# A hybrid decoder layer on one core: QKV weight loads one slot earlier, and the second normalised input turned by VectorE and DRAM instead of TensorE

## The chip, the cores and the metric

The kernel runs on one core of a Trainium2 chip. The metric is the device time of one execution in microseconds (us); lower is better. Engines carry the profile's names: PE (TensorE; PEld is its weight load), DVE (VectorE), ACT (ScalarE), POOL (GpSimd), SP (SyncE, which here only issues DMAs).

## The reference, cut to what matters

One decoder layer over 1024 tokens of 1024 channels, in f32. The first part normalises the input and projects it into a recurrent branch (RG-LRU), three groups of dilated window attention and gates. The part that the change's larger half touches is the end:

```
merged = gates[0] * yr + gates[1] * ya
x = x + merged @ w_out
pe = p @ w_ple
pg = sigmoid(rms_norm(x, norm_ple) @ w_ple_gate + b_ple_gate)
x = x + pg * pe
```

`rms_norm(x, gain)` divides each token's row by its root mean square and multiplies by a gain per channel. The product with `w_ple_gate` contracts over channels, so the normalised input must stand with channels on partitions, while the rows come out of the product with `w_out` with tokens on partitions. Something has to turn it.

## The kernel before, in words

**Products.** Every f32 product is three matmuls of rounded halves (`hi*hi`, `hi*lo`, `lo*hi`; lines 1318, 1322, 1323), accumulated in one PSUM bank. Product number n goes to bank n % 4; PE waits until product n - 4 has been taken out (`bank_free`). Banks 4 to 7 serve the other uses.

**Weights.** SP loads a weight piece (128 rows x 512) into one of four raw buffers. POOL cuts it: L599 writes the rounded high half and L595 the rest into a ring. In the QKV stage the ring has 12 slots, later 16. SP may load piece p when piece p - 4 is cut; POOL may cut into a slot when PE has used what was there. POOL works through the pieces in order, with some other work at fixed places between them.

**QKV stage.** Nine chunks of weights, each 8 pieces, and 8 token tiles per chunk: 72 slots of 8 blocks (a block is one piece's three matmuls). Attention steps are strewn among the blocks, one per 6 blocks. `main_order` writes the order of slots and steps out, and each engine follows it. In step A, DVE rotates and normalises q and k of tile A, transposes them in 32 x 32 squares (L1160) and SP turns them over DRAM: four writes of 32 KB (L542), then, when they have landed, a read of 128 KB (L549). PE uses a tile four steps later. `loaded_after(G)` says up to which piece SP has issued loads when it passes slot G of this order: half the next chunk after the chunk's slot 0, all of it after slot 2. SP's loads (L528, later L504) and turns stand in one order on one queue.

Between the first four and the last four pieces of chunks 3 and 4, POOL permutes half of the first normalised input (`permute_hn`, L615, 16 instructions each), which PE needs in pairs from slot 0 and slot 4 of chunk 3 on.

**The end.** `merged` is held as m_hi and m_lo. The product with `w_out` runs over two halves of the columns, 8 token tiles each (`natural`, 24 matmuls a tile). For each tile of the second half:

- DVE adds x (L1262);
- ACT sums the squares and takes the root (L962, L964);
- DVE takes the reciprocal (L1271) and scales the row by it and the gain into `xg` (L1276), two buffers;
- PE transposes tile t - 2 in eight squares into banks 4 and 5 (`xg_transposes`, L1559);
- ACT copies the banks to m_hi (L954), and DVE writes the rest to m_lo (L1250).

Tiles 6 and 7 are transposed among the first tiles of the last stage. There, for two halves of the columns and 8 tiles each, PE makes a gate product (24 matmuls) and a product with `w_ple` (6 matmuls). DVE adds the bias to the gate product (L1287), ACT takes the sigmoid (L972), DVE multiplies by the other product (L1297, which frees its bank) and adds x (L1299), and ACT issues the output DMA.

Of the kernel before, what the change touches and what calls it, by code (L numbers as in the profile page):

```python
# [12 lines left out]
P = 128  # L13
# [40 lines left out]
PIECES = FIRST_TAIL + PIECES_TAIL  # L54
PIECES_Z = (2 * KD + HEADS) * KD // 4
FIRST_O = FIRST_TAIL + PIECES_Z


def ring_slot(p):
# [52 lines left out]
def loaded_after(G):  # L112

    if G < SLOTS_Q:
        c, s = divmod(G, NT)
        return FIRST_QKV + KD * (c + 1) + (KD // 2 if s < 2 else KD)
    return FIRST_TAIL + max(KD, G - SLOTS_Q + 11)

# [1 line left out]
Q_STAT = 15  # L120

P_CUT = (2, 4)

WARM = 16

# [98 lines left out]
def build_layer(nc, a):  # L224
    stack = ExitStack()
    with stack:
        def sem(name):
            return stack.enter_context(nc.semaphore(name))
# [93 lines left out]
        x2 = [at(f"x2_{t}", [P, D], F32, x2_off[t]) for t in range(NT)]  # L322
        xg = [at("xg0", [P, D], F32, X + 40960), at("xg1", [P, D], F32, H + 45056)]
        gain_ple = at("gain_ple", [P, D], F32, X + 45056)
        pT = at("pT", [P, KP, S], F32, H + 40960)
        pT_hi = at("pT_hi", [P, KP, S], F32R, H + 49152)
        pT_lo = at("pT_lo", [P, KP, S], F32R, H + 57344)
# [25 lines left out]
        y_dram = nc.dram_tensor("y_dram", (NJ, 2, P, S), F32, kind="Internal").ap()  # L353
        o_dram = nc.dram_tensor("o_dram", (UNITS, P, S), F32, kind="Internal").ap()
        gate_dram = nc.dram_tensor("gate_dram", (2 * KD, P, S), F32, kind="Internal").ap()
        turn_dram = nc.dram_tensor("turn_dram", (4, 2 * QUADS, QUAD, QUADS, QUAD), F32, kind="Internal").ap()
        stat_dram = nc.dram_tensor("stat_dram", (2, TILES, P), F32, kind="Internal").ap()
        mw_dram = nc.dram_tensor("mw_dram", (GROUPS, HEADS * NT, P), F32, kind="Internal").ap()
# [96 lines left out]
        x2_std = sem("x2_std")  # L455
        half_done = sem("half_done")
        xg_done = sem("xg_done")
        xgT_done = sem("xgT_done")
        xgT_hi_done = sem("xgT_hi_done")
        xgT_lo_done = sem("xgT_lo_done")  # L460
        pre_done = sem("pre_done")
# [39 lines left out]
        @block.sync  # L501
        def _(sp):
            def load(s, src):
                sp.dma_start(raw[:, s], src).then_inc(raw_in[s], 16)  # L504


            for t in range(4):
                sp.dma_start(x_nat[:, t], a["x"][t * P:(t + 1) * P, :]).then_inc(x_in[t], 16)
            for dst, src in ((ident, "ident"), (gain_mix, "gain_mix")):
                sp.dma_start(dst[:], a[src]).then_inc(consts_in, 16)  # L510
            for s in range(RAW):
                load(s, a["w_rnn_s"][s])
            for t in range(4, NT):
                sp.dma_start(x_nat[:, t], a["x"][t * P:(t + 1) * P, :]).then_inc(x_in[t], 16)
            for dst, src in ((bias_in, "bias_in"), (chan, "chan")):
                sp.dma_start(dst[:], a[src]).then_inc(chan_in, 16)
            sp.dma_start(spare_first[:, :, 0], chunk_bias(0).rearrange("p (q i) -> p q i", q=4)).then_inc(bq_in[0], 16)

            def load_pieces(first, end):

                for p in range(first, end):
                    sp.wait_ge(w_ready, p + 1 - RAW)
                    if p < FIRST_QKV:
                        load(p % RAW, a["w_rnn_s"][p])
                    elif p < FIRST_TAIL:
                        c, k = divmod(p - FIRST_QKV, KD)
                        for u, col, width, dst in chunk_sources(c):
                            sp.dma_start(raw[:, p % RAW, dst:dst + width], a["w_qkv_s"][u * KD + k, :, col:col + width]  # L528
                                         ).then_inc(raw_in[p % RAW], 16)
                    else:  # L530
                        load(p % RAW, a["w_tail_s"][p - FIRST_TAIL])
                return max(first, end)

            def turn_tile(g):

                r, s = g % 2, g % NT
                squares = turn_dram[g % 4]
                sp.wait_ge(qkr_done, g + 1)
                if g >= 4:
                    sp.wait_ge(qkT_in[r], 16 * ((g - 4) // 2 + 1))  # L540
                for i in range(QUADS):
                    sp.dma_start(squares[:, :, i].rearrange("b i j -> i b j"),  # L542
                                 qkr[i * QUAD:(i + 1) * QUAD, r].rearrange("p w a b -> p (w a b)").rearrange(
                                     "p (b j) -> p b j", j=QUAD)).then_inc(turn_out[r], 16)
                sp.wait_ge(turn_out[r], 16 * QUADS * (g // 2 + 1))
                if g >= NT:
                    old = g - NT
                    sp.wait_ge(qk_done, old - old % NT + last_reader(old // (HEADS * NT), old % NT) + 1)
                sp.dma_start(qkT[:, :, s * P:(s + 1) * P],  # L549
                             squares.rearrange("(w b) i a j -> (b i) w (a j)", w=2)).then_inc(qkT_in[r], 16)  # L550

            loaded = load_pieces(RAW, FIRST_QKV + KD)
            for what, G in MAIN_ORDER:
                if what == "slot":
                    loaded = load_pieces(loaded, loaded_after(G))
                elif G < TILES:
                    turn_tile(G)
                if (what, G) == ("step", TILES - 1):
                    break
            load_pieces(loaded, PIECES)  # L560


        @block.gpsimd
# [70 lines left out]
        def _(act):  # L634
# [313 lines left out]
            act.wait_ge(pT_lo_done, KP)  # L948
            act.dma_start(bias_ple[:], a["bias_ple"].to_broadcast([P, D])).then_inc(bple_in, 16)

            def xgT_hi(t):
                act.wait_ge(xgT_done, t + 1)
                for b in range(2):
                    nc.scalar.activation(m_hi[:, 4 * b:4 * b + 4, t * P:(t + 1) * P],  # L954
                                         bank[4 + b][:].rearrange("p (k q) -> p k q", k=4),
                                         ACT.Copy).then_inc(xgT_hi_done, 1)

            for t in range(NT):
                act.wait_ge(x2_done, NT + t + 1)
                if t == 0:  # L960
# [2 lines left out]
                                              accum_out=ssq_x[:, t:t + 1]))  # L963
                nc.scalar.activation(std_x[:, t:t + 1], ssq_x[:, t:t + 1], ACT.Sqrt, bias=half_x[:, t:t + 1],  # L964
                                     scale=1.0 / D).then_inc(x2_std, 1)
                if t >= 2:
                    xgT_hi(t - 2)

            for i in range(2 * NT + 1):
                if i < 2 * NT:  # L970
                    act.wait_ge(pre_done, i + 1)
                    nc.scalar.activation(fin[i % 3][:], fin[i % 3][:], ACT.Sigmoid).then_inc(pg_done, 1)  # L972
                if i < 2:
                    xgT_hi(NT - 2 + i)
                if i >= 1:
                    eh, t = divmod(i - 1, NT)
                    act.wait_ge(fin_done, i)
# [7 lines left out]
        def _(dve):  # L985
# [259 lines left out]


            def xgT_lo(t):
                dve.wait_ge(xgT_hi_done, 2 * t + 2)
                for b in range(2):
                    V.tensor_tensor(m_lo[:, 4 * b:4 * b + 4, t * P:(t + 1) * P],  # L1250
                                    bank[4 + b][:].rearrange("p (k q) -> p k q", k=4),
                                    m_hi[:, 4 * b:4 * b + 4, t * P:(t + 1) * P].bitcast(F32),
                                    ALU.subtract).then_inc(xgT_lo_done, 1)

            for i in range(2 * NT):
                eh, t = divmod(i, NT)
# [9 lines left out]
                    V.tensor_tensor(pT_lo[:, k], pT[:, k], pT_hi[:, k].bitcast(F32), ALU.subtract).then_inc(pT_lo_done, 1)  # L1266
                if eh == 1:
                    if t == 0:
                        dve.wait_ge(gain_in, 16)
                    dve.wait_ge(x2_std, t + 1)  # L1270
                    link(V.reciprocal(rstd_x[:, t:t + 1], std_x[:, t:t + 1]))  # L1271
                    if t >= 2:
                        xgT_lo(t - 2)
                    if t >= 2:
                        dve.wait_ge(xgT_done, t - 1)
                    V.scalar_tensor_tensor(xg[t % 2][:], x2[t][:], rstd_x[:, t:t + 1], gain_ple[:],  # L1276
                                           ALU.mult, ALU.mult).then_inc(xg_done, 1)
            dve.wait_ge(bple_in, 16)
            for i in range(2 * NT + 1):
                if i < 2 * NT:  # L1280
# [4 lines left out]
                    if i >= 3:  # L1285
                        dve.wait_ge(fin_out[i % 3], 16 * (i // 3))
                    V.tensor_tensor(fin[i % 3][:], bank[n % 4][:], bias_ple[:, hs], ALU.add).then_inc(pre_done, 1)  # L1287
                if i < 2:
                    xgT_lo(NT - 2 + i)
                if i >= 1:  # L1290
                    m = i - 1
                    eh, t = divmod(m, NT)
# [10 lines left out]
        def _(pe):  # L1303
# [247 lines left out]
                    elif last_tile:  # L1551
                        ins.then_inc(w_used, 1)

            def xg_transposes(t):
                pe.wait_ge(xg_done, t + 1)
                if t >= 1:
                    pe.wait_ge(xgT_lo_done, 2 * t)
                for k in range(KD):
                    ins = T.transpose(bank[4 + k // 4][:, (k % 4) * P:(k % 4 + 1) * P], xg[t % 2][:, k * P:(k + 1) * P], ident[:])  # L1559
                ins.then_inc(xgT_done, 1)  # L1560

            for i in range(2 * NT):
                eh, t = divmod(i, NT)
                n = N_W + i
# [2 lines left out]
                if eh == 0 and t in (0, NT // 2):  # L1567
                    pe.wait_ge(m_sum, 2 * KD + (KD if t == 0 else 2 * KD))
                natural(n, lambda k: (m_hi[:, k, ts], m_lo[:, k, ts]), first + eh * KD, KD, t == NT - 1)
                if eh == 1 and t >= 2:  # L1570
                    if t == 2:
                        pe.wait_ge(stat_set, 1)
                    xg_transposes(t - 2)
            first += 2 * KD


            for i in range(2 * NT):
# [2 lines left out]
                ts = slice(t * P, (t + 1) * P)  # L1580
                p0 = first + eh * (KD + KP)
                if eh == 0:
                    pe.wait_ge(xgT_lo_done, 2 * t + 2)
                if i == 0:
                    pe.wait_ge(pT_lo_done, KP)
                bank_free(n)
                natural(n, lambda k: (m_hi[:, k, ts], m_lo[:, k, ts]), p0, KD, t == NT - 1)
                bank_free(n + 1)
                natural(n + 1, lambda k: (pT_hi[:, k, ts], pT_lo[:, k, ts]), p0 + KD, KP, t == NT - 1)
                if eh == 0 and t < 2:  # L1590
                    xg_transposes(NT - 2 + t)


# ---- launch: layout of the inputs on the host, one core
# [102 lines left out]
```

## Time and profile before

| | us |
|---|---|
| median of 3 runs | 1331.48 (1330.89 to 1331.71) |
| the profiled execution's own time | 1330.25 |
| its span, first to last instruction | 1328.4 |
| PE busy | 1312.6 |
| POOL busy | 516.8 |
| DVE busy | 736.1 |

The profile is of one execution. Times inside it count from its first instruction. Matmuls are pipelined, so that the time from one to the next (0.23 us for 512 columns) is shorter than the duration shown for one. The share of the DMA engines is a mean over the core's 16.

### The profile page before, as it was taken

The page shows a single profiled execution, that of the slowest core. Times are in us where ns is not written, and L with a number is a line of the kernel's source. Part 1 is how long each engine was busy: PE and PEld are TensorE (multiplying, and loading weights), DVE is VectorE, ACT ScalarE, POOL GpSimd, SP SyncE. Part 2 cuts the span into 40 slices and gives each one's busy share as a digit, 9 for nine tenths or more (in the row PEclk, how much of TensorE's full clock was granted, in tenths as well). Part 3 has the DMA queues.
Part 4 walks back from the last instruction along what each step waited for, and adds up shares of the span by engine and source line. Part 5 has one row for each costly group of instructions (what it writes and reads, how often), then busy time and mean ns, then how long its engine had stood idle before and what let it go on. Part 6 is the DMA issues. An engine that isn't in the chain of part 4 may idle for free.

```text
span 1328.4 us, 17821 instructions
## 1 busy us (share of the span) xinstructions
PE 1312.6 (99%) x6070; PEld 1088.4 (82%) x6070; DVE 736.1 (55%) x1352; ACT 476.5 (36%) x1186; POOL 516.8 (39%) x500
## 2 busy tenths in 40 slices
PE   9999999999999799999999999999999999999998
PEld 6887888888888688888888888888888888888887
DVE  6799888852656365665666551257412457134323
ACT  7455656642324243343442677221100011223100
POOL 7976424404275542222322424341175316045020
PEclk9999999999999999999999999999999999999999
DMA  6232322332354344544535456376279534022111
GB/s 249 77 107 80 98 77 80 108 104 75 69 129 101 83 108 108 135 102 105 133 90 131 119 150 181 110 246 229 79 293 407 190 123 166 40 80 64 40 40 48
DMA packets 215386, 164.72 MB, mean 124 GB/s; under 512 B 116448, under 2 KB 172032, under 8 KB 215296
## 3 DMA queue, kind: packets, MB, share of 16 engines
q1 hardware_dynamic: 175008, 87.76, 24.4%
q10 hardware_dynamic: 40288, 75.82, 16.1%
q8 instruction: 49, 0.80, 0.3%
q14 instruction: 41, 0.34, 0.1%
HBM read 121.42 MB, written 42.09 MB: 123 GB/s over the span
## 4 chain that ended last, share of the span: by engine, by line
PE 91%; DVE 4%; POOL 2%; ACT 1%; DMA 1%; issue 0%; SPq 0%; POOLq 0%; ACTq 0%
PE bank L1318 28%; PE bank L1323 28%; PE bank L1322 28%; PE bank L1466 2%; PE bank L1446 2%; POOL hn L615 1%; PE bank L1455 1%; DVE xc L1048 1%; PE bank L1559 1%; PE bank L1363 0%; DMA gain_mix<-in_gain_mix 0%; POOL ring L595 0%; DVE ibuf L1075 0%; DVE tbuf L1067 0%; DVE y_lo L1084 0%
## 5 line engine op out<-in xcount | busy, mean ns | idle before, releaser
L599 POOL TENSOR_SCALAR ring<-raw 128x512 fp32r<-128x512 f32 x221 | 161.4, 730 | 726.7 <-PE bank L1323 516.1
L595 POOL TENSOR_TENSOR ring<-raw,ring 128x512 fp32r<-128x512 f32 x221 | 315.3, 1427 | 18.4
L1318 PE MATMUL bank<-hn,ring 128*128 128x512 f32 x640 | 252.0, 394 | 1.6 <-DVE sgbuf L1036 1.2
L1323 PE MATMUL bank<-hn,ring 128*128 128x512 f32 x640 | 249.4, 390 | 0.0
L1322 PE MATMUL bank<-hn,ring 128*128 128x512 f32 x640 | 249.0, 389 | 0.0
L1318 PE MATMUL bank<-ring,hn 128*128 128x512 f32 x576 | 233.6, 406 | 6.8 <-POOL hn L615 6.8
L1323 PE MATMUL bank<-ring,hn 128*128 128x512 f32 x576 | 226.0, 392 | 0.0
L1322 PE MATMUL bank<-ring,hn 128*128 128x512 f32 x576 | 225.6, 392 | 0.0
L1318 PEld LDWEIGHTS bank<-hn,ring 128*128 128x128 f32 x640 | 120.2, 188 | 26.9 <-DVE sgbuf L1036 1.6
L1323 PEld LDWEIGHTS bank<-hn,ring 128*128 128x128 f32 x640 | 120.1, 188 | 25.5
L1322 PEld LDWEIGHTS bank<-hn,ring 128*128 128x128 f32 x640 | 120.3, 188 | 24.0
L1318 PEld LDWEIGHTS bank<-ring,hn 128*128 128x128 f32 x576 | 109.8, 191 | 28.9 <-POOL hn L615 9.2
L1323 PEld LDWEIGHTS bank<-ring,hn 128*128 128x128 f32 x576 | 109.5, 190 | 23.4
L1322 PEld LDWEIGHTS bank<-ring,hn 128*128 128x128 f32 x576 | 110.0, 191 | 19.9
L1121 DVE CUSTOM_DVE_ANT_0 scores<-bank,masks 128x128 f32<-128x128 f32 (+1 forms) x96 | 33.6, 350 | 140.3 <-PE bank L1446 140.3
L1318 PE MATMUL bank<-ring,m_hi 128*128 128x512 f32 x256 | 100.3, 392 | 0.0
L1323 PE MATMUL bank<-ring,m_lo 128*128 128x512 f32 x256 | 99.7, 389 | 0.0
L1322 PE MATMUL bank<-ring,m_hi 128*128 128x512 f32 x256 | 99.6, 389 | 0.0
L751 ACT ACTIVATE spare_last<-qkv 128x128 f32<-128x128 f32 x130 | 38.9, 300 | 140.3 <-DVE qkv L1026 140.3
L1026 DVE TENSOR_TENSOR qkv<-bank,bias_qkv 128x512 f32<-128x512 f32 x64 | 43.5, 680 | 73.8 <-PE bank L1323 73.8
L786 ACT ACTIVATE scores<-scores,neg_max 128x128 f32<-128x128 f32 (+1 forms) x96 | 43.1, 449 | 86.3 <-DVE neg_max L1121 86.0
L1048 DVE SCALAR_TENSOR_TENSOR xc<-x_pad,chan,xc 128x512 f32<-128x512 f32 x60 | 59.7, 995 | 11.0 <-ACT xc L691 9.6
(180 smaller groups left out, 2057.8 us busy)
## 6 DMA issues: line engine op xcount, KB each, us to landing
raw<-in_w_tail_s SPq DMA_DIRECT2D x104, 256.0 KB, 3.1
turn_dram<-qkr SPq DMA_DIRECT2D x384, 32.0 KB, 1.8
qkT<-turn_dram SPq DMA_DIRECT2D x96, 128.0 KB, 2.1
g_in<-gate_dram ACTq DMA_DIRECT2D x48, 256.0 KB, 3.6
raw<-in_w_rnn_s SPq DMA_DIRECT2D x45, 256.0 KB, 2.6
raw<-in_w_qkv_s SPq DMA_DIRECT2D x48, 192.0 KB, 2.8
gate_dram<-g_out ACTq DMA_DIRECT2D x32, 256.0 KB, 2.2
raw<-in_w_qkv_s SPq DMA_DIRECT2D x48, 128.0 KB, 2.7
```

The source lines that it names most:

```text
L595: nc.gpsimd.tensor_tensor(ring[:, ring_slot(p), 1], raw[:, p % RAW], ring[:, ring_slot(p), 0].bitcast(F32), ALU.subtract).then_inc(w_ready, 1)
L599: nc.gpsimd.tensor_scalar(ring[:, ring_slot(p), 0], raw[:, p % RAW], 1.0, 1.0, ALU.mult, ALU.mult).then_inc(hi_cut, 1)
L751: ins = nc.scalar.activation((spare_first[:, i, 1] if T < PERM_FREE else spare_last[:, i, 0]), qkv[:, c % 3, s, b], ACT.Square, accum_out= ...
L786: nc.scalar.activation(scores[:, g % 2, c0:], scores[:, g % 2, c0:], ACT.Exp, scale=-1.0, bias=neg_max[:, col:col + 1], accum_out=den[:, c ...
L1026: V.tensor_tensor(qkv[:, c % 3, s], by_tile(bank[(N_A + T) % 4][:]), by_tile(bias_qkv[:, c % 2]) if c else spare_first[:, :, 0], ALU.add). ...
L1048: ins = V.scalar_tensor_tensor(xc[:, b, hs], shifted(k), chan[:, k, j:j + 1], xc[:, b, hs], ALU.mult, ALU.add)
L1121: V.tensor_tensor_reduce(out=scores[:, g % 2, c0:], in0=bank[5][:, c0:2 * P], in1=masks[:, c0:2 * P] if grp < 2 else masks[:, 2 * P:], sca ...
L1318: ins = T.matmul(out, lhs[0], rhs[0], start=first, stop=False)
L1322: T.matmul(out, lhs[0], rhs[1], start=False, stop=False)
L1323: return T.matmul(out, lhs[1], rhs[0], start=False, stop=last)
L1446: T.matmul(bank[5][:, 0 if prev else P:2 * P], qkT[:, 0, tile * P:(tile + 1) * P], keys, start=True, stop=True).then_inc(qk_done, 1)
L1466: ins = T.matmul(bank[7][:, 0:P], qkv[:, c % 3, tile if b else prev_tile(grp, tile), vb], probsT[:, g % 2, b * P:(b + 1) * P], start=b == ...
```

## The change

1. `loaded_after(G)` reckons the chunk and slot from G + 1 instead of G for the QKV stage, so the same pieces are issued one slot earlier in SP's order.
2. PE's 64 transposes go. The gain is copied by ACT into banks 4 and 5. DVE scales a tile in two halves from there, and transposes it in place in 32 x 32 squares. SP writes it to DRAM in four DMAs of 128 KB (32 partitions x 32 runs of 128 bytes each) and reads it back turned in one DMA of 512 KB (runs of 512 bytes) into one buffer `xgT`. ACT's copy to m_hi and DVE's subtraction to m_lo now read `xgT`, one instruction each instead of two, three tiles behind instead of two.
3. SP issues the write of tile t + 1 ahead of the read of tile t. Write t waits for read t - 2 (two DRAM buffers); a read waits for its write and for the subtraction of the tile before. The last weight loads are put among these.

```
 def loaded_after(G):
     if G < SLOTS_Q:
-        c, s = divmod(G, NT)
+        c, s = divmod(G + 1, NT)
...
+LAG_XG = 3
...
 # SP
-            load_pieces(loaded, PIECES)
+            load_pieces(loaded, FIRST_PG + RAW)
+            for t in range(NT + 1):
+                if t < NT:
+                    if t < 2:
+                        load_pieces(FIRST_PG + RAW * (t + 1), FIRST_PG + RAW * (t + 2))
+                    sp.wait_ge(xg_done, t + 1)
+                    if t >= 2:
+                        sp.wait_ge(xgT_in, 16 * (t - 1))
+                    for i in range(QUADS):
+                        sp.dma_start(xgt_dram[t % 2, :, :, i].rearrange("b i j -> i b j"),
+                                     xg[t % 2][i * QUAD:(i + 1) * QUAD].rearrange("p (b j) -> p b j", j=QUAD)
+                                     ).then_inc(xg_out[t % 2], 16)
+                if t >= 1:
+                    r = t - 1
+                    sp.wait_ge(xg_out[r % 2], 16 * QUADS * (r // 2 + 1))
+                    if r == 0:
+                        sp.wait_ge(gain_set, 2)
+                    else:
+                        sp.wait_ge(xgT_lo_done, r)
+                    sp.dma_start(xgT[:], xgt_dram[r % 2].rearrange("(k b) i a j -> (b i) k (a j)", b=QUADS)
+                                 ).then_inc(xgT_in, 16)
+            load_pieces(FIRST_PG + 3 * RAW, PIECES)
...
 # ACT
+            for eh in range(2):
+                nc.scalar.activation(bank[4 + eh][:], gain_ple[:, eh * HALF:(eh + 1) * HALF],
+                                     ACT.Copy).then_inc(gain_set, 1)
             def xgT_hi(t):
-                act.wait_ge(xgT_done, t + 1)
-                for b in range(2):
-                    nc.scalar.activation(m_hi[:, 4 * b:4 * b + 4, t * P:(t + 1) * P],
-                                         bank[4 + b][:].rearrange("p (k q) -> p k q", k=4),
-                                         ACT.Copy).then_inc(xgT_hi_done, 1)
+                act.wait_ge(xgT_in, 16 * (t + 1))
+                nc.scalar.activation(m_hi[:, :, t * P:(t + 1) * P], xgT[:], ACT.Copy).then_inc(xgT_hi_done, 1)
...
 # DVE, per tile of the second half
-                    if t >= 2:
-                        xgT_lo(t - 2)
-                    if t >= 2:
-                        dve.wait_ge(xgT_done, t - 1)
-                    V.scalar_tensor_tensor(xg[t % 2][:], x2[t][:], rstd_x[:, t:t + 1], gain_ple[:],
-                                           ALU.mult, ALU.mult).then_inc(xg_done, 1)
+                    if t >= 2:
+                        dve.wait_ge(xg_out[t % 2], 16 * QUADS * (t // 2))
+                    for b in range(2):
+                        bs = slice(b * HALF, (b + 1) * HALF)
+                        ins = V.scalar_tensor_tensor(xg[t % 2][:, bs], x2[t][:, bs], rstd_x[:, t:t + 1], bank[4 + b][:],
+                                                     ALU.mult, ALU.mult)
+                    link(ins)
+                    V.transpose(xg[t % 2][:], xg[t % 2][:]).then_inc(xg_done, 1)
+                    if t >= LAG_XG:
+                        xgT_lo(t - LAG_XG)
...
 # DVE, last stage, per tile i: after the bias is added to the gate product
-                if i < 2:
-                    xgT_lo(NT - 2 + i)
+                if i < LAG_XG:
+                    xgT_lo(NT - LAG_XG + i)
...
 # PE, second half of the w_out product and first tiles of the last stage
-                if eh == 1 and t >= 2:
-                    if t == 2:
-                        pe.wait_ge(stat_set, 1)
-                    xg_transposes(t - 2)
...
-                    pe.wait_ge(xgT_lo_done, 2 * t + 2)
+                    pe.wait_ge(xgT_lo_done, t + 1)
...
-                if eh == 0 and t < 2:
-                    xg_transposes(NT - 2 + t)
```

## Rows read from the trace of the kernel before

**Rows 1.** The page, part 1: busy time, share of the span, instructions.

```profile
PE 1312.6 (99%) x6070; PEld 1088.4 (82%) x6070; DVE 736.1 (55%) x1352; ACT 476.5 (36%) x1186; POOL 516.8 (39%) x500
```

**Rows 2.** Waits of PE: us in total, times, longest us.

```profile
PE bank L1318 <- POOL hn L615: 6.8, 6, 1.4
```

**Rows 3.** Timeline of POOL, 366 to 455 us; in brackets idle time before.

```profile
408.92 1.29 POOL L595 TENSOR_TENSOR ring<-raw,ring 128x512 fp32r<-128x512 f32 x1
423.44 0.62 POOL L599 TENSOR_SCALAR ring<-raw 128x512 fp32r<-128x512 f32 x1 [13.23 <-DMA raw<-in_w_qkv_s]
...
431.29 18.84 POOL L615 TENSOR_SCALAR hn<-hn 128x512 fp32r<-128x512 f32 x16
```

**Rows 4.** Timeline of SP, 403.7 to 424.5 us: start, duration, line.

```profile
403.85 0.38 SPq L549 DMA_DIRECT2D qkT<-turn_dram  x1
406.35 1.78 SPq L542 DMA_DIRECT2D turn_dram<-qkr  x4
409.35 0.38 SPq L549 DMA_DIRECT2D qkT<-turn_dram  x1
411.44 1.81 SPq L542 DMA_DIRECT2D turn_dram<-qkr  x4
...
416.49 1.78 SPq L542 DMA_DIRECT2D turn_dram<-qkr  x4
...
419.91 3.84 SPq L528 DMA_DIRECT2D raw<-in_w_qkv_s  x8
```

**Rows 5.** Timeline of ACT, 1100 to 1330 us: two tiles of either product.

```profile
1159.70 0.60 ACT L940 ACTIVATE bank<-x 128x512 f32<-128x512 f32 x1 [4.39 <-DVE x L1262]
...
1165.14 0.60 ACT L940 ACTIVATE bank<-x 128x512 f32<-128x512 f32 x1 [4.39 <-DVE x L1262]
...
1282.49 0.63 ACT L972 ACTIVATE fin<-fin 128x512 f32<-128x512 f32 x1 [6.17 <-DVE fin L1287]
...
1289.29 0.63 ACT L972 ACTIVATE fin<-fin 128x512 f32<-128x512 f32 x1 [6.17 <-DVE fin L1287]
```

**Rows 6.** The chain that ended last: start, duration; PE's turns.

```profile
1180.63 0.87 PE bank L1559 x8
1186.98 0.87 PE bank L1559 x8
...
1220.07 0.87 PE bank L1559 x8
1227.80 0.87 PE bank L1559 x8
```

**Rows 7.** Timeline of DVE, 1166 to 1186 us: one tile.

```profile
1180.67 0.69 DVE L1262 TENSOR_TENSOR x<-bank,x 128x512 f32<-128x512 f32 x1 [2.15 <-PE bank L1323]
1182.47 0.16 DVE L1271 RECIPROCAL rstd_x<-std_x 128x1 f32<-128x1 f32 x1 [1.12 <-ACT std_x L964]
```

**Rows 8.** Groups by line and form, 1090 to 1330 us.

```profile
L1266 DVE TENSOR_TENSOR pT_lo<-pT,pT_hi 128x1024 fp32r<-128x1024 f32 x2 | 2.5, 1226 | 4.1 <-ACT pT_hi L947 4.1
...
L947 ACT ACTIVATE pT_hi<-pT 128x1024 fp32r<-128x1024 f32 x2 | 2.1, 1044 | 0.0
```

**Rows 9.** Groups by line and form, whole span: busy us, mean ns.

```profile
L1160 DVE STREAM_TRANSPOSE qkr<-qks 128x256 f32<-128x256 f32 x96 | 42.8, 446 | 5.1 <-DMA turn_dram<-qkr 1.9
...
L1155 DVE TENSOR_TENSOR qks<-bank,cossin 128x256 f32<-128x256 f32 x96 | 40.7, 424 | 3.3
```

**Rows 10.** Windows; last two columns are DMA share and GB/s.

```profile
404.80:405.70 0.90, 0.90 (x6) 0.73 (x5) 0.86 (x3) 0.04 (x1) 0.82 (x2) 1.00 0.51 146
406.30:409.30 3.00, 3.00 (x18) 2.55 (x17) 1.20 (x5) 0.46 (x3) 2.83 (x5) 1.00 0.26 44
407.14:407.50 0.36, 0.36 (x4) 0.28 (x3) 0.00 (x0) 0.00 (x0) 0.36 (x1) 1.00 0.54 91
407.50:407.62 0.12, 0.12 (x2) 0.12 (x1) 0.00 (x0) 0.00 (x0) 0.12 (x1) 1.00 0.00 0
```

**Rows 11.** DMA issues by line: KB each, us to landing.

```profile
qkT<-turn_dram SPq DMA_DIRECT2D x96, 128.0 KB, 2.1
```

More of the change, by code:

```diff
@@ L56 @@
 FIRST_O = FIRST_TAIL + PIECES_Z
+FIRST_PG = PIECES - 2 * (KD + KP)
 def ring_slot(p):
@@ L324, in build_layer @@
         gain_ple = at("gain_ple", [P, D], F32, X + 45056)
+        xgT = at("xgT", [P, KD, P], F32, X + 45056)
         pT = at("pT", [P, KP, S], F32, H + 40960)
@@ L355, in build_layer @@
         gate_dram = nc.dram_tensor("gate_dram", (2 * KD, P, S), F32, kind="Internal").ap()
+        xgt_dram = nc.dram_tensor("xgt_dram", (2, D // QUAD, QUAD, QUADS, QUAD), F32, kind="Internal").ap()
         turn_dram = nc.dram_tensor("turn_dram", (4, 2 * QUADS, QUAD, QUADS, QUAD), F32, kind="Internal").ap()
@@ L457, in build_layer @@
         xg_done = sem("xg_done")
-        xgT_done = sem("xgT_done")
+        gain_set = sem("gain_set")
+        xg_out = [sem("xg_out0"), sem("xg_out1")]
+        xgT_in = sem("xgT_in")
         xgT_hi_done = sem("xgT_hi_done")
@@ L949, in _ @@
             act.dma_start(bias_ple[:], a["bias_ple"].to_broadcast([P, D])).then_inc(bple_in, 16)
-            def xgT_hi(t):
-                act.wait_ge(xgT_done, t + 1)
-                for b in range(2):
-                    nc.scalar.activation(m_hi[:, 4 * b:4 * b + 4, t * P:(t + 1) * P],
-                                         bank[4 + b][:].rearrange("p (k q) -> p k q", k=4),
-                                         ACT.Copy).then_inc(xgT_hi_done, 1)
+            act.wait_ge(gain_in, 16)
+            act.wait_ge(stat_set, 1)
+            for eh in range(2):
+                nc.scalar.activation(bank[4 + eh][:], gain_ple[:, eh * HALF:(eh + 1) * HALF],
+                                     ACT.Copy).then_inc(gain_set, 1)
+            def xgT_hi(t):
+                act.wait_ge(xgT_in, 16 * (t + 1))
+                nc.scalar.activation(m_hi[:, :, t * P:(t + 1) * P], xgT[:], ACT.Copy).then_inc(xgT_hi_done, 1)
             for t in range(NT):
@@ L965, in _ @@
                                      scale=1.0 / D).then_inc(x2_std, 1)
-                if t >= 2:
-                    xgT_hi(t - 2)
+                if t >= LAG_XG:
+                    xgT_hi(t - LAG_XG)
             for i in range(2 * NT + 1):
@@ L972, in _ @@
                     nc.scalar.activation(fin[i % 3][:], fin[i % 3][:], ACT.Sigmoid).then_inc(pg_done, 1)
-                if i < 2:
-                    xgT_hi(NT - 2 + i)
+                if i < LAG_XG:
+                    xgT_hi(NT - LAG_XG + i)
                 if i >= 1:
@@ L1247, in xgT_lo @@
             def xgT_lo(t):
[L1248 to L1253, printed above, removed]
+                dve.wait_ge(xgT_hi_done, t + 1)
+                V.tensor_tensor(m_lo[:, :, t * P:(t + 1) * P], xgT[:], m_hi[:, :, t * P:(t + 1) * P].bitcast(F32),
+                                ALU.subtract).then_inc(xgT_lo_done, 1)
             for i in range(2 * NT):
@@ L1268, in _ @@
                     if t == 0:
-                        dve.wait_ge(gain_in, 16)
+                        dve.wait_ge(gain_set, 2)
                     dve.wait_ge(x2_std, t + 1)
@@ L1272, in _ @@
                     if t >= 2:
-                        xgT_lo(t - 2)
-                    if t >= 2:
-                        dve.wait_ge(xgT_done, t - 1)
-                    V.scalar_tensor_tensor(xg[t % 2][:], x2[t][:], rstd_x[:, t:t + 1], gain_ple[:],
-                                           ALU.mult, ALU.mult).then_inc(xg_done, 1)
+                        dve.wait_ge(xg_out[t % 2], 16 * QUADS * (t // 2))
[5 more added lines that the diff above has]
+                    V.transpose(xg[t % 2][:], xg[t % 2][:]).then_inc(xg_done, 1)
+                    if t >= LAG_XG:
+                        xgT_lo(t - LAG_XG)
             dve.wait_ge(bple_in, 16)
@@ L1287, in _ @@
                     V.tensor_tensor(fin[i % 3][:], bank[n % 4][:], bias_ple[:, hs], ALU.add).then_inc(pre_done, 1)
-                if i < 2:
-                    xgT_lo(NT - 2 + i)
+                if i < LAG_XG:
+                    xgT_lo(NT - LAG_XG + i)
                 if i >= 1:
@@ L1552, in natural @@
                         ins.then_inc(w_used, 1)
[L1554 to L1560, printed above, removed]
             for i in range(2 * NT):
```

## The prediction

> **What bounds the kernel now.** I read the page's engine shares first: TensorE (PE) is busy for 99% of the span [rows 1]. So a change pays only by taking work off PE or by ending a PE wait, and costs only by making one. PE's waits come next: one group is worth naming, 6.8 us in six waits of at most 1.4 us on POOL's L615, the permuted copy of the first normalised input [rows 2]. In the timelines of POOL and SP the reader is to see why L615 was late. POOL had cut its last piece at 410.21 and then sat idle for 13.23 us until raw weights landed [rows 3]; SP issued those loads only at 419.91, behind the turns of two attention tiles, and the second of these had been waiting for VectorE [rows 4]. The permute stands behind these four pieces in POOL's order and needs 18.84 us.
>
> For the second part I read the pace of the end. T0 is 1164.3, where PE starts the second half of the output product: the last add of the first half, 0.69 us long, stands between it and the square at 1165.14 [rows 5]. Each of its 8 tiles is 5.44 us of matmuls, and each tile of the last product 6.80 us [rows 5], of which 24 of 30 matmuls, 5.44 us, make the gate product. Where PE also turns a tile, the spacing is 6.35 instead of 5.44, and 7.73 instead of 6.80 [rows 6].
>
> **The change, part by part.**
>
> 1. *Loads one slot ahead.* One slot spans eight blocks, and the steps of tiles 17 and 18 lie in the slot that the load now passes. SP is free after the read at 409.35, at 409.7; the ring condition of the last load is met at 410.21 [rows 3, 4]. The eight DMAs then take 409.8 to 413.7 instead of 419.91 to 423.75, so POOL starts 3.5 us after the first issue, as now, near 413.3 rather than 423.44, and the permute near 421 rather than 431.29. It ends near 440. PE now gets its last pair at 450.13; without the 6.8 us of waiting it would want it at 443.4. So all six waits go: **-6.8 us**; the ends are -6.8 and 0 (no move). What is queued behind the load on SP: the turn of tile 17 goes out at 413.7 instead of 411.44. PE uses a tile four steps, some 20 us, later, and VectorE's double buffer comes round after two; 2.3 us is covered. At other chunk edges SP waits for cuts for a few us, under the same cover.
>
> 2. *PE loses 64 transposes.* Six tiles at 6.35 - 5.44 = 0.91 and two at 7.73 - 6.80 = 0.93: **-7.3 us** if nothing new waits.
>
> 3. *VectorE.* Per tile it does: add 0.69, gap to the reciprocal 1.12, reciprocal 0.16 [rows 7]; the scaling in two halves from PSUM, each taken like the add, 0.69; the 1024-wide transpose; the subtract, now from SBUF, 1.23 [rows 8]. The transpose is not there at this size: it takes 0.446 at 256 columns, an f32 product of 256 columns 0.424 [rows 9] and the add of 512 columns 0.69, so 256 columns more cost 0.27 and the transpose is put at 0.446 + 3 x 0.27 = 1.25; upper end 4 x 0.446 = 1.8, lower end one add, 0.69. With 0.3 for links the sum is 0.69 + 1.12 + 0.16 + 1.38 + 1.25 + 1.23 + 0.3 = 6.1 us, above PE's 5.44. VectorE no longer hides by itself.
>
> 4. *The DRAM turn.* Per tile, 4 writes with 1024 packets of 128 B each, and a read of 1024 packets of 512 B. In the attention turn 1024 packets of 128 B take 0.26 x 3.0 x 16 engines = 12.5 us, 12.2 ns each; 256 of 512 B take 0.51 x 0.9 x 16 = 7.3 us, 28.7 ns [rows 10]. So a new write is 64 x 4 x 12.2 ns = 3.1, say **3.2 us**, and a read 64 x 28.7 ns = 1.8, say **2.0 us** with its ramp. Bounds of the write: 3.1, and four times what 128 KB needs at most, from the first packet at 407.14 to the read's issue at 409.35 [rows 4, 10] less 0.35 for landing, 4 x 1.86 = 7.4 us. I take the lower end, because within one 32 KB write the share is 0.54 and between two it is 0.00 [rows 10]: there SP's issue sets the pace. The read lies between 1.8 and 3.6 (four times the 0.9 us of 128 KB). The Trainium skill ("DMA: Bandwidth & Descriptors", section Specifications) asks for transfers of 512 B or more for the full rate and says that smaller ones become a read-modify-write. The trace agrees in direction: 10.5 GB/s per engine at 128 B against 17.8 at 512 B; that is already in the 12.2 ns.
>
>    The waits set the loop. Write t+2 is issued when read t has landed, and read t+1 queues behind it on SP's DMA queue: lead from issue to first packet 0.8 [rows 4, 10] + 3.2 + 2.0 + 0.35 of landing (a 128 KB read lands 2.1 us after issue, 1.0 lead and 0.8 to 0.9 moving [rows 4, 10, 11]) = **p = 6.35 us** per tile. ScalarE's copy of 1.04 [rows 8] and the subtract lie beside the next write.
>
> 5. *The deadline.* VectorE's iteration 3 begins when PE ends tile 3, T0 + 21.8, and runs 6.1 us: the first subtract ends at T0 + 28.0. (Its read is there: tile 1 is turned by T0 + 16.6, its write ends near 21, and read 0 behind it lands near 23.5.) The others follow at p. In the last product VectorE puts the subtract of tile 6 ahead of the multiply that frees a bank for PE's third tile. That multiply ends at 28.0 + 6p + 0.8 = 66.9; PE wants the bank at 43.5 + 2 x 6.80 + 5.44 = 62.6. The stall is 6p - 33.8 = **+4.3 us**. One tile (6.8 us) on, the subtract of tile 7 gives 28.0 + 7p + 0.8 - 69.4 = 7p - 40.6 in total, which leads once p is above 6.8. The tiles' own subtracts are ready in time in both.
>
> 6. *Edits with no term.* ScalarE's two gain copies precede its first square of this half; weight loads put among the writes move 1 MB in VectorE's first two iterations, and the last eight, issued after the last read near T0 + 70, are wanted at T0 + 98; POOL's cuts for them still follow PE's use.
>
> **Sum:** -6.8 - 7.3 + 4.3 = -9.8 on the profiled execution's 1330.25 us: 1320.4. The median shown is 1.2 higher, so 1321.7.
>
> **Rivals.**
> - *The small-packet writes become the bound* (slower side). Mechanism: long runs of 128 B packets keep the pace of the 7.4 us end. Then p = 0.8 + 7.4 + 2.0 + 0.35 = 10.55, the stall is 7p - 40.6 = 33, and the time 1331.5 - 14.1 + 33 = 1350. It decides from a stall of 14.1, p = 7.8, a write of 4.7 us. For it: nothing in the trace runs 4096 such packets in a row; against: the empty stretches between writes. 18%.
> - *In between*, write or read a fifth to a half dearer, or the transpose at 1.8: p of 6.7 to 7.8, stall 6 to 14, time 1324 to 1331. 14%.
> - *No stall at all*: VectorE's last intervals are shorter, since no scaling stands between the subtracts there: 1331.5 - 14.1 = 1317.4. 8%.
> - *The load doesn't move the permute*, because SP is held ahead of it: 1331.5 - 7.3 + 4.3 = 1328.5. SP's free time at 409.7 speaks against it. 8%.
> - *Forecast* as summed, 1318 to 1324: 52%.
>
> If PE idles for several us its clock might drop; the longest of the waits listed is 1.4 us [rows 2], so I give it no term and leave it to the upper side. The Trainium skill ("TensorE: Matmul & The Clock Gate", Part 1) says that an idle TensorE is throttled to 1.2 GHz.
>
> **How the numbers follow.** A measurement here can tell about 0.2%, 2.7 us, from no change. Faster by more: the forecast, the case without a stall, most of the case in between and part of the unmoved load, 0.72. Same: the top of the case in between, the unmoved load's upper half and the edge of the slow rival, 0.11. Slower: the slow rival and a little of the unpriced, 0.17. The range reaches from 1316.5 (no stall, both savings) to 1337, a stall of 19.6 at p = 8.6, a write of 5.4 us; beyond it lies about two thirds of the slow rival.
>
> **What would show it.** Right: no PE wait on L615; POOL's first cut after 410 starts near 413; no L1559; one PE wait of 3 to 5 us at the third tile of the last product, behind VectorE's multiply; reads about 6.3 us apart. Wrong: writes that take over 4.7 us of packets, PE waits of 10 us there, or a new PE wait on the attention turn after the earlier loads.

## The result, and the profile after

The changed kernel takes 1322.07 us (median of 4 runs, 1321.72 to 1323.42), the kernel before beside it 1331.6: a ratio of 0.9933, interval 0.9921 to 0.9945. That is 9.5 us less, against 9.8 forecast. The sum came out; two of its three terms did not, and their errors went opposite ways.

The page's first part shows PE just as busy, with 64 fewer matmuls:

```profile
PE 1305.4 (99%) x6006; PEld 1082.7 (82%) x6006; DVE 746.2 (57%) x1360; ACT 478.4 (36%) x1180; POOL 517.0 (39%) x500
```

PE's waits (us in total, times, longest) no longer name the permute [rows 2]. The longest is now a single one on DVE's multiply, which is L1329 in the changed kernel and was L1297:

```profile
PE bank L1350 <- DVE fin L1329: 6.4, 1, 6.4
PE bank L1419 <- POOL warm L617: 1.3, 1, 1.3
```

**The loads.** SP's timeline (start, duration, line) shows the eight loads right behind a read, where [rows 4] had them behind two turns:

```profile
409.54 0.38 SPq L556 DMA_DIRECT2D qkT<-turn_dram  x1
409.96 4.06 SPq L535 DMA_DIRECT2D raw<-in_w_qkv_s  x8
414.12 3.04 SPq L549 DMA_DIRECT2D turn_dram<-qkr  x4
```

POOL's timeline answers [rows 3]: 4.06 us idle instead of 13.23, and the permute starts at 422.30 instead of 431.29.

```profile
409.12 1.28 POOL L623 TENSOR_TENSOR ring<-raw,ring 128x512 fp32r<-128x512 f32 x1
414.46 0.62 POOL L627 TENSOR_SCALAR ring<-raw 128x512 fp32r<-128x512 f32 x1 [4.06 <-DMA raw<-in_w_qkv_s]
...
422.30 18.95 POOL L643 TENSOR_SCALAR hn<-hn 128x512 fp32r<-128x512 f32 x16
```

ACT's timeline tells what this was worth further down. The last square of the first half of the output product starts at 1155.50, where [rows 5] have 1165.14: the second half begins 9.6 us earlier, not 6.8.

```profile
1155.50 0.60 ACT L968 ACTIVATE bank<-x 128x512 f32<-128x512 f32 x1 [4.39 <-DVE x L1290]
```

The windows of the kernel before say why. Their last columns are granted clock, DMA share and GB/s. The first window ends 0.3 us before the last of the six waits does, and up to there the clock was 1.00; then for 3.2 us it was 0.50, which is the lower of the two levels, 1.2 GHz:

```profile
438.00:449.90 11.90, 5.92 (x23) 3.58 (x23) 2.59 (x8) 1.63 (x9) 11.07 (x11) 1.00 0.32 73
449.90:453.10 3.20, 2.92 (x7) 2.34 (x8) 0.69 (x1) 0.51 (x3) 0.23 (x1) 0.50 0.00 0
```

PE's timeline of the same kernel shows the matmul ahead of the last wait and the first ones behind it:

```profile
448.41 0.40 PE L1323 MATMUL bank<-ring,hn 128*128 128x512 f32 x1
450.18 0.79 PE L1318 MATMUL bank<-ring,hn 128*128 128x512 f32 x1 [1.38 <-POOL hn L615]
450.77 0.63 PE L1322 MATMUL bank<-ring,hn 128*128 128x512 f32 x1
451.20 0.63 PE L1323 MATMUL bank<-ring,hn 128*128 128x512 f32 x1
```

Seven matmuls from 450.18 on stand some 0.43 us apart instead of 0.23, 1.5 us more in all. Each of the six waits also hides the 0.16 us by which a matmul's row (0.39) outlasts the spacing (0.23), 1.0 us in all. 6.8 + 1.0 + 1.5 = 9.3. The first matmul behind each of the other five waits takes 0.34 us to the next instead of 0.23, 0.5 us more: 9.8. That is the whole gain, since the changed execution stood 0.2 us behind at the start of this stretch (SP's read at 409.54 for 409.35) and was 9.6 us ahead at the end.

**The turn.** SP's timeline of the last stage but one shows the loop of writes (L576) and reads (L586):

```profile
1180.36 2.24 SPq L576 DMA_DIRECT2D xgt_dram<-xg  x4
1183.01 0.38 SPq L586 DMA_DIRECT2D xgT<-xgt_dram  x1
1187.07 2.23 SPq L576 DMA_DIRECT2D xgt_dram<-xg  x4
1189.41 0.56 SPq L586 DMA_DIRECT2D xgT<-xgt_dram  x1
1193.57 2.24 SPq L576 DMA_DIRECT2D xgt_dram<-xg  x4
1196.75 0.38 SPq L586 DMA_DIRECT2D xgT<-xgt_dram  x1
1201.05 2.24 SPq L576 DMA_DIRECT2D xgt_dram<-xg  x4
...
1209.95 0.55 SPq L586 DMA_DIRECT2D xgT<-xgt_dram  x1
```

From read 1 (1183.01) to read 5 (1209.95) there are four steps of 6.7 us on average, 6.35 having been forecast. The writes are issued 6.7, 6.5 and then 7.5 us apart. Two windows, the packets of one write and of the read behind it (DMA share and GB/s last), give the terms: a write takes 2.75 us and not 3.2, a read 2.55 and not 2.0; together 5.3, forecast 5.2. Per packet that is 1.16 x 2.75 x 16 / 4096 = 12.5 ns at 128 B and 0.75 x 2.55 x 16 / 1024 = 29.9 ns at 512 B, as in [rows 10].

```profile
1187.85:1190.60 2.75, 2.75 (x14) 2.28 (x13) 2.09 (x3) 0.86 (x3) 0.00 (x0) 1.00 1.16 189
1190.70:1193.25 2.55, 2.55 (x13) 2.10 (x12) 1.86 (x4) 0.30 (x1) 0.00 (x0) 1.00 0.75 205
```

DVE's two new sizes, in the groups by line and form (busy us, mean ns), are 1.36 for the subtract (1.23 forecast) and 1.25 for the transpose, as forecast. The longest subtract took 2.04; the read at 1196.75 goes out when it ends, and that is the long step of 7.5:

```profile
L1280 DVE TENSOR_TENSOR m_lo<-xgT,m_hi 128x1024 fp32r<-128x1024 f32 x8 | 10.9, 1357 | 14.6 <-ACT m_hi L987 14.6
...
L1307 DVE STREAM_TRANSPOSE xg<-xg 128x1024 f32<-128x1024 f32 x8 | 10.0, 1245 | 0.3
```

```profile
1194.63 2.04 DVE L1280 TENSOR_TENSOR m_lo<-xgT,m_hi 128x1024 fp32r<-128x1024 f32 x1 [0.42 <-ACT m_hi L987]
```

Now the deadline. In DVE's timeline the first subtract ends at 1182.62, the seventh (tile 6) at 1222.94, and the multiply behind it at 1223.53:

```profile
1181.39 1.23 DVE L1280 TENSOR_TENSOR m_lo<-xgT,m_hi 128x1024 fp32r<-128x1024 f32 x1
...
1221.71 1.23 DVE L1280 TENSOR_TENSOR m_lo<-xgT,m_hi 128x1024 fp32r<-128x1024 f32 x1 [4.58 <-ACT m_hi L987]
1222.85 0.68 DVE L1329 TENSOR_TENSOR fin<-bank,fin 128x512 f32<-128x512 f32 x1
```

With T0 = 1154.7 (0.8 before the square above) the first is at T0 + 27.9, 28.0 forecast, and the seventh at T0 + 68.2, where the forecast had 66.1. PE's timeline shows the price: the last matmul ahead of the wait starts at 1216.84, the next at 1223.59, and the ones after it stand 0.43 apart until 1228.45.

```profile
1216.84 0.39 PE L1355 MATMUL bank<-ring,m_lo 128*128 128x512 f32 x1
1223.59 0.79 PE L1350 MATMUL bank<-ring,pT_hi 128*128 128x512 f32 x1 [6.37 <-DVE fin L1329]
1224.18 0.63 PE L1354 MATMUL bank<-ring,pT_hi 128*128 128x512 f32 x1
...
1228.45 0.45 PE L1355 MATMUL bank<-ring,m_lo 128*128 128x512 f32 x1
```

The wait costs 6.75 - 0.23 = 6.5 us. Then 11 matmuls take 4.86 us instead of 2.5, another 2.4. The windows (granted clock third from the end) show the lower level there, and 1.00 where the permute used to be waited for:

```profile
438.00:456.00 18.00, 18.00 (x93) 15.18 (x92) 10.19 (x31) 6.17 (x31) 3.08 (x3) 1.00 0.36 79
1216.90:1223.50 6.60, 0.33 (x2) 0.00 (x0) 2.02 (x3) 1.69 (x2) 0.00 (x0) 0.87 0.44 105
1223.50:1228.30 4.80, 4.71 (x11) 3.74 (x12) 1.33 (x3) 1.69 (x2) 0.38 (x1) 0.50 0.79 256
```

So by the trace the second part of the change is worth -7.3 + 6.5 + 2.4 = +1.6 us: as built it costs a little, and the whole gain is the loads'. Runs 1 and 2 put this to the test.

### The profile page after: what moved, and what is told of

The parts are those of the page before. It is cut to its first block, busy times and chain, and to the rows that moved or that the text cites. A ratio compares the mean times of both kernels' runs of the same rounds, so it can differ in the third digit from the quotient of the medians.

```text
span 1320.4 us, 17742 instructions
## 1 busy us (share of the span) xinstructions
PE 1305.4 (99%) x6006; PEld 1082.7 (82%) x6006; DVE 746.2 (57%) x1360; ACT 478.4 (36%) x1180; POOL 517.0 (39%) x500
## 4 chain that ended last, share of the span: by engine, by line
PE 89%; DVE 5%; DMA 3%; ACT 1%; SPq 1%; issue 1%; DVEq 0%; ACTq 0%
PE bank L1350 28%; PE bank L1355 28%; PE bank L1354 28%; PE bank L1498 2%; PE bank L1478 2%; DMA xgT<-xgt_dram 2%; PE bank L1487 1%; DVE xc L1079 1%; SPq L576 1%; DVE m_lo L1280 1%; PE bank L1395 0%; DMA gain_mix<-in_gain_mix 0%; ACT m_hi L987 0%; DVE ibuf L1106 0%; DVE y_lo L1115 0%
```

## The experiments

The theory after reading the trace was this. The earlier loads are worth 9.6 us, waits and clock together. The turn itself is a small loss, because PE waits for one bank behind a late subtract that it doesn't need yet, and pays again in clock. The chip times beside each run are those of the kernel before on the same chip.

**1. The loads alone.** The kernel before with one line changed:

```
-        c, s = divmod(G, NT)
+        c, s = divmod(G + 1, NT)
```

> The kernel before with the loads one slot ahead and nothing else. Theory (waits and clock): the six waits on the permute go, 6.8 us, and with them the stretch at half clock that followed the last of them (granted clock 0.50 from about 450 to 453 us in the kernel before) and the lost overlap at each wait; together 9.6 us, so 1331.6 - 9.6 = 1322.0 us. Rival (waits alone, as the prediction had it): 6.8 us, 1324.8 us.

1320.63 us against 1331.42, a ratio of 0.992 (0.9905 to 0.9936), so 8.5 to 12.6 us less. The waits alone (6.8) lie outside. PE's list of waits holds nothing above 0.3 us but the start of the kernel; its first two entries:

```profile
PE bank L1387 <- POOL warm L589: 1.3, 1, 1.3
PE bank L1318 <- DVE sgbuf L1036: 1.1, 1, 1.1
```

By medians this one line is 1.4 us faster than the whole change, though the two intervals overlap. The fifteen runs of the kernel before on this chip set the clock apart from the waits: the only one with a mean granted clock of 1.000 took 1328.85 us, 8.2 more than the loads alone, and the eleven at 0.996 took 1330.96 to 1332.21. So of the 10.8 us by medians some 8 go with the waits and their edges, and some 2.6 with the clock; the profiled execution, with 1.5 for the clock, was one of the milder ones.

**2. The turn alone.** The changed kernel with that line put back.

> The changed kernel with the loads put back: only the turn by VectorE and DRAM. Theory: -7.3 us of transposes, +6.5 of the wait behind the subtract of tile 6, +2.4 of matmuls at half clock after it, together +1.6, so 1333.2 us, no faster than the kernel before. Rival (the prediction's terms): -7.3 + 4.3 = -3.0, 1328.6 us.

1332.58 against 1331.42, a ratio of 1.0011 (1.0002 to 1.002): a loss of 0.3 to 2.7 us. The prediction's -3.0 for these terms is excluded. Both waits are there:

```profile
PE bank L1350 <- POOL hn L643: 6.6, 6, 1.4
PE bank L1350 <- DVE fin L1329: 5.3, 1, 5.3
```

**3. The multiply first.** The changed kernel; DVE's order in the last stage, per tile i:

```
-                if i < LAG_XG:
-                    xgT_lo(NT - LAG_XG + i)
                 if i >= 1:
...
                     V.tensor_tensor(fin[m % 3][:], fin[m % 3][:], x2[t][:, hs], ALU.add).then_inc(fin_done, 1)
+                if i < LAG_XG:
+                    xgT_lo(NT - LAG_XG + i)
```

> The changed kernel; in the last stage VectorE multiplies (and adds x) first and subtracts the late tile after it. Theory (the wait is VectorE's order, not DRAM's pace): of the 6.5 us about 0.9 is left, the clock stays up, and the time falls by 8 us against the changed kernel, to 1314. Rival (the turned tiles come too late for PE itself): the wait moves to the tile's own subtract, 1320 to 1322.

1314.72, a ratio of 0.9876 (0.9863 to 0.989), clear of the changed kernel's. The tiles were in time for PE; what was late was a multiply in the queue behind them. PE's waits keep 1.6 us on that multiply, since the subtract of tile 5 still stands ahead of it (the last line number is the multiply's here), and 0.9 us on the first bias add behind the subtract of tile 4. The granted clock stayed at 1.00 after both:

```profile
PE bank L1350 <- DVE fin L1327: 1.6, 1, 1.6
```

**4. The subtracts a tile later still.** In the same place, with the multiply first:

```
-                if i < LAG_XG:
-                    xgT_lo(NT - LAG_XG + i)
+                if 1 <= i <= LAG_XG:
+                    xgT_lo(NT - LAG_XG + i - 1)
```

> The changed kernel with VectorE's multiply first and the last three subtracts one tile later than in the run with the multiply first. Theory: the 1.6 us of PE wait left there go, since the bank of the first tile is then freed ahead of any late subtract, and nothing new waits: 1313. Rival: a tile comes too late for PE's own need, a wait on the subtract appears at the sixth to eighth tile and the time is 1315 or more.

1313.11 against 1330.96, a ratio of 0.9865 (0.985 to 0.988). It is the fastest version of this study, and 7.5 us below the loads alone by medians (7.1 if each is taken against the kernel before on its own chip), about the 7.3 of the transposes. Its longest waits are those of the kernel's start:

```profile
PE bank L1395 <- DMA gain_mix<-in_gain_mix: 1.5, 1, 1.5
PE bank L1419 <- POOL warm L617: 1.3, 1, 1.3
```

**5. A filler for the clock.** The changed kernel; PE runs matmuls that nobody reads while it would wait:

```
+                if i == 2:
+                    for _ in range(27):
+                        T.matmul(bank[6][:], m_hi[:, 0, 0:P], part(p0)[0], start=True, stop=True)
                 bank_free(n + 1)
```

> The changed kernel; PE runs 27 matmuls into an unused bank, 6.1 us, while it would wait behind the third tile of the last product. They take part in no output. Theory: the clock stays at 1.00 after the wait and 2.4 us come back, 1319.7. Rival (the clock fall costs nothing): unchanged, 1322.1; or slower if the filler runs past the wait.

1319.92. The difference from the changed kernel is small beside the intervals of runs on different chips, so both ran once more side by side.

> The changed kernel once more, beside the next two on one chip: 1322 us by every theory.

> The filler of 27 matmuls once more, now beside the changed kernel on the same chip. Theory: 2.2 to 2.4 us below it, since the granted clock stays at 1.00 after the wait. Rival: no difference beyond 1 us.

1322.38 (0.9924 to 0.9948) without and 1320.19 (0.9907 to 0.9934) with the filler: 2.2 us by medians. The intervals against the kernel before overlap, but the ranges of the five runs, 1321.8 to 1323.82 and 1319.79 to 1321.28, do not. The same 5 us after the wait, in windows of both, show the cause. The first bracket counts PE's matmuls; third from the end is the granted clock. First the changed kernel:

```profile
1224.00:1229.00 5.00, 5.00 (x13) 3.87 (x13) 1.41 (x3) 1.69 (x2) 0.83 (x2) 0.52 0.91 302
```

and the one with the filler, with 23 matmuls in the same time:

```profile
1224.00:1229.00 5.00, 5.00 (x23) 4.13 (x22) 1.52 (x3) 1.70 (x2) 0.90 (x2) 1.00 0.85 293
```

PE does 27 matmuls more and the kernel is faster.

**6. A DRAM buffer for each tile.** The changed kernel, where no write waits for a read any more:

```
-        xgt_dram = nc.dram_tensor("xgt_dram", (2, D // QUAD, QUAD, QUADS, QUAD), F32, kind="Internal").ap()
+        xgt_dram = nc.dram_tensor("xgt_dram", (NT, D // QUAD, QUAD, QUADS, QUAD), F32, kind="Internal").ap()
...
-                    if t >= 2:
-                        sp.wait_ge(xgT_in, 16 * (t - 1))
...
-                        sp.dma_start(xgt_dram[t % 2, :, :, i].rearrange("b i j -> i b j"),
+                        sp.dma_start(xgt_dram[t, :, :, i].rearrange("b i j -> i b j"),
...
-                    sp.dma_start(xgT[:], xgt_dram[r % 2].rearrange("(k b) i a j -> (b i) k (a j)", b=QUADS)
+                    sp.dma_start(xgT[:], xgt_dram[r].rearrange("(k b) i a j -> (b i) k (a j)", b=QUADS)
```

> The changed kernel with a DRAM buffer for each tile, so that no write waits for a read. Theory (two loops of nearly one length: write and read on one queue, about 6.4 us, and read, ScalarE's copy, subtract, read, also about 6.6 us): the second still holds, the period stays within 0.3 us of 6.7, and the time within 2 us of the changed kernel, 1320 to 1324. Rival (the write's wait for the read alone sets the period, as the prediction had it): the period falls to VectorE's 6.1, the wait at the third tile by 3 to 4 us, and the time to 1316 to 1318.

1321.88, a ratio of 0.993 (0.9918 to 0.9943): no change. SP's reads stand 6.5 us apart:

```profile
1190.49 0.38 SPq L584 DMA_DIRECT2D xgT<-xgt_dram  x1
...
1197.01 0.38 SPq L584 DMA_DIRECT2D xgT<-xgt_dram  x1
...
1203.54 0.38 SPq L584 DMA_DIRECT2D xgT<-xgt_dram  x1
```

So the wait that the prediction held for the loop's only cause was one of two of nearly one length. Without it, read, ScalarE's copy and subtract carry the period: each of these reads is issued 0.1 us after a subtract ends, and DVE waits 0.7 to 1.0 us for the copy ahead of the subtract. The period is 0.2 us shorter than in the changed kernel, but the first subtract ends 1.2 us later after T0, so that the wait at the end is no shorter (6.6 us).

**7. The read ahead of the next write.** The changed kernel with SP's new order undone:

```
-            for t in range(NT + 1):
+            for t in range(NT):
...
-                if t >= 1:
-                    r = t - 1
+                if True:
+                    r = t
```

> The changed kernel with SP's order undone: the read of tile t ahead of the write of tile t + 1. Theory: a read then lands about 3.9 us after its issue instead of 4.1, and the write goes behind it and still lands before the next read is wanted (1.0 + 2.5 + 2.8 + 0.35 = 6.65 us); the period stays near 6.7 and the time within 2 us of the changed kernel. Rival (the order hides the write): each tile pays write and read one after the other, 3.9 + 4.1 + 2.4 = 10.4 us, the wait at the end grows by over 20 us, and the time is 1340 or more.

1344.87 against 1330.96, a ratio of 1.0102 (1.0088 to 1.0116). My expectation fell: with DVE's order as it is, SP's order is worth 22.8 us by medians. The rival had the time about right. Reads are 11.1 us apart:

```profile
1209.52 0.38 SPq L586 DMA_DIRECT2D xgT<-xgt_dram  x1
1209.99 4.12 SPq L576 DMA_DIRECT2D xgt_dram<-xg  x4
1220.59 0.38 SPq L586 DMA_DIRECT2D xgT<-xgt_dram  x1
```

But DVE's waits showed a third way, which neither had named: it waits ahead of its scaling (L1304) for the write that frees one of its two row buffers.

```profile
DVE xg L1304 <- DMA xgt_dram<-xg: 26.3, 5, 5.6
```

Write t + 1 now goes out behind read t, which waits for the subtract of tile t - 1; on DVE that subtract stands behind the scaling of tile t + 2, and this scaling waits for write t. So each tile pays in a circle: subtract, read and write on the queue, scaling, transpose, subtract.

**8. The subtract ahead of the scaling.** Run 7 with DVE's order changed, nothing else:

```
+                    if t >= LAG_XG:
+                        xgT_lo(t - LAG_XG)
                     if t >= 2:
                         dve.wait_ge(xg_out[t % 2], 16 * QUADS * (t // 2))
...
-                    if t >= LAG_XG:
-                        xgT_lo(t - LAG_XG)
```

> The read ahead of the next write, as in the run that lost 22.8 us, and on VectorE the subtract of tile t - 3 ahead of the scaling of tile t. Theory formed from that run (VectorE waits 5.3 us per tile, ahead of its scaling, for the write that frees the buffer of the rows; the subtract stands behind that wait, and the next read behind the subtract): the subtract no longer waits for a write, reads are issued about 7 us apart instead of 11, and the time falls back to 1320 to 1326. Rival (write and read one after the other on the queue are the period, whatever VectorE's order): reads stay 11 us apart and the time stays at 1343 or more.

1323.6, a ratio of 0.9944 (0.9931 to 0.9958). Reads are 7.1 us apart in the steps shown (7.2 and 7.8 before them), with SP's order as in run 7:

```profile
1204.76 0.38 SPq L586 DMA_DIRECT2D xgT<-xgt_dram  x1
...
1211.86 0.38 SPq L586 DMA_DIRECT2D xgT<-xgt_dram  x1
...
1218.94 0.38 SPq L586 DMA_DIRECT2D xgT<-xgt_dram  x1
```

The circle through DVE was the cause: opening it gave 21.3 of the 22.8 us back. What is left over the changed kernel's medians is 1.2 to 1.5 us. That is not the price of the queue's order alone, since DVE's order differs too; the subtract ahead of the scaling with SP's order as changed was not run.

## Why the prediction was right or wrong

- **Total and direction**: 1322.07 for 1321.7, inside the range, but in part by luck. The terms in the traces are -9.6 - 7.3 + 6.5 + 2.4 = -8.0, which is what the two profiled executions differ by (1330.25 and 1322.25): the loads brought 2.8 us more than forecast, and the end cost 4.6 us more. The medians differ by 9.5, mostly because the profiled execution of the kernel before lay 1.2 us below its median.
- **Step 1, the loads (-6.8)**: the mechanism was right, each time of it within 1.3 us (first cut 414.46 for 413.3, permute 422.30 for 421). The term was undersized: it measured 9.6 in the trace and 8.5 to 12.6 in run 1. It counted the listed idle time alone. The half-clock stretch behind the waits was in the trace and got no term, since the longest single wait was 1.4 us.
- **Step 2, the transposes (-7.3)**: right. Run 4 gets 7.1 to 7.5 over run 1 once nothing waits.
- **Step 3, VectorE (6.1)**: right; transpose 1.25 for 1.25, and 6.15 us from the add to the end of the first subtract.
- **Step 4, the DRAM turn (p = 6.35)**: 6.7. Write and read together were right, each off by half a microsecond the other way. That write and read are the loop was half right: run 6 takes the write's wait away and the period stays within 0.2 us. The copy and the subtract, which the prediction put beside the next write, form a loop with the read that is about as long, and the late subtract of 2.04 us made one step 7.5.
- **Step 5, the deadline (+4.3)**: place and cause right, the multiply behind the subtract of tile 6, and 6.5 us for 4.3. Six periods of 0.35 us more are the 2.1. Run 3 shows that the order on DVE, and not the pace over DRAM, decides.
- **The clock**: given no term and left to the upper side, because the waits listed were short, although the sum itself forecast a single wait of 4.3 us. It cost 2.4 us after the wait in the trace; run 5 and its repeat give 2.2 back. By the Trainium skill ("TensorE: Matmul & The Clock Gate", Part 1) an idle TensorE is throttled to 1.2 GHz. The traces agree: 0.50 granted at the end of one wait of 6.5 us, and at the end of six short ones with matmuls between them.
- **The rivals**: the small-packet writes did not become the bound: 4096 such packets in a row took 12.5 ns each, where runs of 256 had taken 12.2. By the Trainium skill ("DMA: Bandwidth & Descriptors", Specifications) runs under 512 B go as read-modify-write. The trace agrees in direction, 10.2 GB/s per engine at 128 B against 17.1 at 512 B; that the writes are read-modify-writes no run shows. That the load wouldn't move fell as well, and so did the case without a stall. The case in between had the pace and the stall (6.7 and 6.5, at its lower end), and missed the time because the loads brought more.

## What to carry to other kernels

A PE wait costs its length and sometimes the clock after it (after 6.5 us here, and after six short waits close together, but not after the 0.9 and 1.6 us of run 3): look at the granted clock in the microseconds behind it, and price both. When an engine works in order, ask of each late operand not only whether its reader can wait, but what stands behind it on the engine that prepares it; here the turn cost 1.6 us by the trace with the subtract first, gained some 6 over the loads alone with a multiply moved ahead of it (run 3), and some 7 with the subtracts a tile later still (run 4). A double buffer that is freed by a DMA belongs to the loop of that DMA's queue: follow the circle through every engine before judging the order of a queue.

## What was not expected of the hardware

- Six PE waits of at most 1.4 us, with 0.7 us of matmuls between most of them, ended with the granted clock at 0.50 for 3.2 us. It was 1.00 until shortly before the last of them ended; in the trace of run 2 it fell before that wait began.
- Four writes of 1024 packets of 128 B, one behind the other, moved 189 GB/s over 2.75 us at a DMA share of 1.16, little under the 205 GB/s of the 512-byte read behind them, whose share was 0.75.
- The order of two DMAs on one queue changed the time by 22.8 us (run 7); 21.3 us of it came back with another engine's program order (run 8).
